# Two norm boundaries of a two-layer kernel in another order: three and four chunks token tile by token tile, three weight chunks split early, no subtraction on POOL

## The chip, the cores and the metric

The kernel runs on one core of a Trainium2 chip. The metric is the device time of one execution in microseconds (us), lower is better. The engines are TensorE (PE), VectorE (DVE), ScalarE (ACT), GpSimd (POOL) and SyncE (SP, which issues all DMAs here).

## What is computed

Two transformer-like layers on 256 tokens of width 2048, in fp32. Cut to what matters:

```python
# first block
h = rms_norm(x, norm_mix_pre)
proj = h @ w_in                        # 2048 x 10240
oa, on = diff_attention(...), neighbourhood_attention(...)
mixed = g_a * (oa @ w_branch_a) + g_b * (on @ w_branch_b)
x = x + rms_norm(mixed @ w_out, norm_mix_post)      # norm boundary 1
u = square(relu(rms_norm(x, norm_mlp_pre) @ w_up))  # 2048 x 8192
x = x + rms_norm(u @ w_down, norm_mlp_post)         # norm boundary 2
# second block
proj = rmsnorm(x, norm_w_2) @ w_in_2
h = x + concat(mlstm(...), hgrn2(...)) @ w_out_2
h = h + sigmoid(rmsnorm(h, pe_norm_w_2) @ w_pg_2) * (p @ w_pe_2)
out = rmsnorm(h, final_norm_w_2)
```

## The kernel before

**Chunks and halves.** All large products are cut into 340 chunks, numbered in the order in which they run. A chunk is four 128-row pieces of a weight matrix by 512 columns (344 in some): 1 MB. Tokens stand in two tiles of 128, t = 0 and 1. A block of chunks (4 of them for 2048 rows, 16 for w_down) sums into two PSUM buffers `acc`, one for each tile. `products(n)` runs chunk n for tile 0 and then for tile 1; such a part is called (n,t) or a half below. The stages start at chunks 0 (w_in), 80 (branches), 96 (w_out, `N_WO`), 112 (w_up, `N_UP`), 176 (w_down, `N_DN`), 240 (second w_in, `N_IN2`), 308, 324.

**fp32 from fp32r.** Each operand is split into a high part, which is a copy rounded to fp32r, and a low part, the difference. A half is 4 x 3 matmuls: hi x ath, lo x ath, hi x atl, where hi/lo belong to the weights and ath/atl to the activations.

**The weight pipeline.** SP loads chunk n into one of three `raw` buffers once the lo of chunk n-3 is made. ACT makes hi (`high(n)`, L461), DVE makes lo (`low(n)`, L811), both into one of three buffers that the products of chunk n-3 have left. ACT and DVE do this for chunk n+2 (`LEAD`) while chunk n runs. Eight lo are made on POOL (`POOL_LO`, L379): those of chunks 3 and 5, 114 to 116, 242 to 244.

**The norm boundaries.** After the last chunk of w_out (111) or w_down (239) the residual stream is renewed: ACT squares the last block (`square`), DVE sums and POOL takes the root (`row_mean`, `root`), DVE weighs the last block (`weigh_last`) and adds a quarter row of a tile at a time to `xs` (`add_row`, L799). Then come eight units (g, t), a group g of 512 columns of tile t: PE turns it around with four transpositions (L1252), DVE scales it by the norm's gain (`unit`, L791), ACT makes ath (L478) and DVE atl (`unit_low`, L836). Units are called r1 at boundary 1 and r2 at boundary 2. `fill` puts them one half ahead of the first chunks of the next stage: chunk 112+g needs units (g,0) and (g,1). Behind the first unit PE runs 16 short matmuls on constants (`warm`). Two chunks later ACT squares the whole rows for the next norm.

**w_down.** Its activations lie in `UT` (64 pieces of 256 columns in `m`). ACT and DVE split four pieces for each chunk (`cut(i)` for chunk 176+i, three chunks ahead).

**Order and waits.** Each engine runs a list written out by hand. Waits are on semaphores that count: a wait for one result is a wait for everything counted before it on that engine.

Of the kernel before, what the change touches and what calls it, by code (L numbers as in the profile page):

```python
# [15 lines left out]
P = 128  # L16
D = 2048
# [10 lines left out]
POOL_LO = {n + i for n in (N_UP, N_IN2) for i in (2, 3, 4)} | {3, 5}  # L28
# [41 lines left out]
def program(nc, x, w_in, w_a, w_b, w_out, w_up, w_down, w_in2, w_out2, w_pg, w_pe, p2,  # L70
            cols, lamv, rpb, rows, bif, cos_c, sin_c, nam_c, id_c, lvl_c, caus_c, out):
    with ExitStack() as ctx:
# [12 lines left out]
        M = sb("m", [P, 80 * KB])  # L85
        SM = sb("sm", [P, 3 * KB])
# [16 lines left out]
        s_plo = Count(sem("s_weights_lo_pool"))  # L103
# [6 lines left out]
        counts = [s_prod, s_pe, s_hi, s_lo, s_plo, s_ach, s_act, s_dve, s_pool, s_out, *s_raw]  # L110
# [103 lines left out]

        def freed(b):

            kind, j = blocks[b][:2]
            return s_dve if kind in on_dve or (kind, j) == ("dn", 3) else s_act

        def view(t, n):  # L220
            return t[n % NRAW][:, 0:4 * chunks[n][1]]

        def lo_done(n):
            return s_plo if n in POOL_LO else s_lo
# [46 lines left out]
        def fill(name, c0):  # L271
            order = [(g, t) for g in range(4) for t in range(2)]
            for i, u in enumerate(order):
                at = max(0, i - 1)
                before.setdefault((c0 + at // 2, at % 2), []).append((name, *u))

# [6 lines left out]
        fill("r1", N_UP)  # L283
        fill("r2", N_IN2)
# [9 lines left out]
        freeing = {"heads": N_AB - 4, "mix": N_WO - 4, "y": N_RES - 4, "pg": N_PG - 4}  # L294

        def taken(name, g):

            return {"r1": N_UP - 1, "r2": N_IN2 - 1}.get(name, freeing.get(name, 0) + g)
# [7 lines left out]
        def sync(e):  # L306
# [5 lines left out]
            def raw(n):  # L312
                if n >= NRAW:
                    sp.wait_ge(lo_done(n - NRAW), "lo", n - NRAW)
                e.dma_start(view(RAW, n).rearrange("p (k c) -> p k c", c=chunks[n][1]), chunks[n][0]).then_inc(
                    s_raw[n % NRAW].on("raw", n), 16)
# [19 lines left out]
            for n in range(3, N_ALL):  # L336
# [34 lines left out]
        def gpsimd(e):  # L371
            po = Queue(e)

            def low(n):
                hi, lo, raw = view(HI, n), view(LO, n), view(RAW, n)
                po.wait_ge(s_hi, "hi", n)
                if n >= NSPL:
                    po.wait_ge(s_prod, "products", n - NSPL, 1)
                e.tensor_tensor(lo, raw, hi.bitcast(F32), ALU.subtract).then_inc(s_plo.on("lo", n))  # L379

# [19 lines left out]
            for n in range(N_ALL):  # L400
                if n == 3:
                    root(2, 2, "r0")
                if n + LEAD in POOL_LO:
                    low(n + LEAD)
# [43 lines left out]
        def scalar(e):  # L448
# [8 lines left out]
            def high(n):  # L457
                if n >= NSPL:
                    ac.wait_ge(s_prod, "products", n - NSPL, 1)
                ac.wait_ge(s_raw[n % NRAW], "raw", n)  # L460
                e.activation(view(HI, n), view(RAW, n), ACT.Copy).then_inc(s_hi.on("hi", n))  # L461

            def unit(name, g, t):
                h = ATH[:, 4 * g:4 * g + 4, t * P:(t + 1) * P]
                if name == "heads":
                    ac.wait_ge(s_act, *(("da back", 7) if g < 2 else ("na out", 7)))
                    ac.wait_ge(s_prod, "products", taken(name, g), 1)
                    src = (QT if g < 2 else QN)[:, 4 * (g % 2):4 * (g % 2) + 4, t * P:(t + 1) * P]
                elif name == "mix":
                    ac.wait_ge(s_pe, "unit", name, g, t)  # L470
                    ac.wait_ge(s_prod, "products", taken(name, g), 1)
                    src = cut4(mis[:, place.get((name, g, t), 0), :])
                else:
                    ac.wait_ge(s_dve, "unit", name, g, t)
                    if name != "x":
                        ac.wait_ge(s_prod, "products", taken(name, g), 1)
                    src = cut4(STG[name][(2 * g + t) % 2])
# [141 lines left out]

            def evac(b):  # L620
                kind, j, n, ids = blocks[b]
                ps = [acc[:, 2 * (b % 2) + t, 0:n] for t in range(2)]
                for t in range(2):
# [16 lines left out]
                    if kind == "wo" or (kind, j) == ("dn", 3):  # L640
# [103 lines left out]
            for n in range(N_ALL):  # L744
                for t in range(2):
# [3 lines left out]
                if n + LEAD < N_ALL:  # L749
                    high(n + LEAD)  # L750
# [9 lines left out]
                if n in (N_UP + 3, N_IN2 + 3):  # L760
# [817 lines left out]
```

## Time and profile before

| | us |
|---|---|
| median of 3 runs | 2049.67 |
| lowest, highest | 2048.22, 2049.98 |
| profiled execution, own time | 2048.93 |
| its span in the trace | 2047.1 |
| PE busy | 2007.7 (98%) |
| DVE busy | 1180.9 (58%) |
| ACT busy | 981.8 (48%) |
| POOL busy | 77.2 (4%) |

Times in the views are counted from the start of the span. A line of the timeline gives start, duration, engine, source line, operation, out<-in, shapes, and in brackets the idle time of the engine before it and what ended that. Matmuls are pipelined: their durations overlap, so the distance of two starts tells their cost, not the duration.

### The profile page before, as it was taken

The numbers are of one execution on the slowest core, as the hardware profiler recorded it, in microseconds if no ns is written. First come the engines' busy times: TensorE is split into PE (matmuls) and PEld (weight loads), VectorE is DVE, ScalarE is ACT, GpSimd is POOL, SyncE is SP. The second block draws the span as 40 slices with busy tenths as digits, with TensorE's granted clock in tenths as the row PEclk, the third lists the DMA queues.
The fourth block names the chain that finished last, engine by engine and source line by source line (L and its number), as shares of the span: only waits on it lengthen the run. The fifth ranks groups of instructions, "written<-read, shape, count | busy, mean of one in ns | idle before, by whom it ended". The sixth has DMA issues, their size and how long they took to land.

```text
span 2047.1 us, 22415 instructions
## 1 busy us (share of the span) xinstructions
PE 2007.7 (98%) x9288; PEld 1664.1 (81%) x9288; DVE 1180.9 (58%) x1067; ACT 981.8 (48%) x956; POOL 77.2 (4%) x50
## 2 busy tenths in 40 slices
PE   7999999999999899999999999999999999999998
PEld 6888888888888688888888888887789888888776
DVE  5655546644655644444456666676567858676554
ACT  4335544445444354444455555553555445444443
POOL 2000000000000200000000000001100000230000
PEclk9999999999999999999999999999999999999999
DMA  6554455555646465656555555564446444465442
GB/s 229 201 199 145 164 188 183 174 185 188 223 164 206 124 193 183 185 185 189 183 181 203 186 196 195 185 226 144 165 144 207 165 152 152 133 221 191 158 166 108
DMA packets 184894, 366.79 MB, mean 179 GB/s; under 512 B 6616, under 2 KB 13400, under 8 KB 184152
## 3 DMA queue, kind: packets, MB, share of 16 engines
q1 hardware_dynamic: 184792, 365.36, 53.7%
q8 instruction: 73, 1.20, 0.2%
q14 instruction: 29, 0.24, 0.0%
HBM read 363.24 MB, written 2.10 MB: 178 GB/s over the span
## 4 chain that ended last, share of the span: by engine, by line
PE 95%; DVE 2%; issue 2%; ACT 1%; DMA 0%; POOL 0%; SPq 0%; DVEq 0%; POOLq 0%; ACTq 0%
PE acc L1249 88%; PE mis L1249 4%; PE mis L1252 3%; DVE xs L799 1%; DVE m L791 1%; DVE atl L836 0%; DMA xs<-in_x 0%; POOL lo L379 0%; ACT hi L461 0%; DVE xs L791 0%; ACT ath L478 0%; ACT sm L455 0%; ACT m L454 0%; SPq L310 0%; DVE m L799 0%
## 5 line engine op out<-in xcount | busy, mean ns | idle before, releaser
L811 DVE TENSOR_TENSOR lo<-raw,hi 128x2048 fp32r<-128x2048 f32 (+1 forms) x331 | 750.5, 2269 | 661.0 <-ACT hi L461 658.9
L1249 PE MATMUL acc<-hi,ath 128*128 128x512 f32 (+1 forms) x2720 | 1073.6, 395 | 8.9 <-DVE atl L836 8.9
L1249 PE MATMUL acc<-hi,atl 128*128 128x512 f32 (+1 forms) x2720 | 1056.7, 388 | 0.0
L1249 PE MATMUL acc<-lo,ath 128*128 128x512 f32 (+1 forms) x2720 | 1055.7, 388 | 0.0
L461 ACT ACTIVATE hi<-raw 128x2048 fp32r<-128x2048 f32 (+1 forms) x339 | 640.1, 1890 | 403.3 <-PE acc L1249 402.7
L1249 PEld LDWEIGHTS acc<-hi,ath 128*128 128x128 f32 x2720 | 513.0, 189 | 113.2 <-DVE atl L836 7.8
L1249 PEld LDWEIGHTS acc<-hi,atl 128*128 128x128 f32 x2720 | 512.6, 188 | 105.3
L1249 PEld LDWEIGHTS acc<-lo,ath 128*128 128x128 f32 x2720 | 513.4, 189 | 100.3 <-issue 0.5
L454 ACT ACTIVATE m<-mis 128x512 f32<-128x512 f32 (+1 forms) x96 | 50.3, 524 | 222.8 <-PE mis L1252 193.9
L454 ACT ACTIVATE m<-acc,st 128x512 f32<-128x512 f32 (+1 forms) x102 | 69.3, 679 | 112.4 <-PE acc L1249 109.4
L791 DVE TENSOR_TENSOR m<-m 128x512 f32<-128x512 f32 (+2 forms) x117 | 74.2, 634 | 22.8 <-ACT m L454 18.1
L1249 PE MATMUL mis<-m 128*128 128x128 f32 (+1 forms) x492 | 84.3, 310 | 0.0
L478 ACT ACTIVATE ath<-m 128x512 fp32r<-128x512 f32 x48 | 29.8, 629 | 113.0 <-DVE m L791 102.2
L843 DVE TENSOR_TENSOR atl<-m,ath 128x1024 fp32r<-128x1024 f32 x64 | 78.0, 1219 | 5.4 <-ACT ath L485 5.4
L384 POOL TENSOR_TENSOR st<-st,mhalf 128x1 f32<-128x1 f32 (+3 forms) x20 | 17.3, 863 | 1686.1 <-DVE st L795 1686.1
L1249 PEld LDWEIGHTS mis<-m 128*128 128x128 f32 x492 | 68.6, 191 | 4.7
L485 ACT ACTIVATE ath<-m 128x1024 fp32r<-128x1024 f32 x64 | 66.7, 1042 | 2.1 <-PE acc L1249 2.1
L454 ACT ACTIVATE m<-m 128x1024 f32<-128x1024 f32 (+3 forms) x34 | 36.0, 1058 | 62.0 <-DVE m L791 58.8
L1252 PE MATMUL mis<-idn,m 128*128 128x128 f32 x356 | 54.2, 272 | 4.3 <-DVE m L791 4.0
L1252 PEld LDWEIGHTS mis<-idn,m 128*128 128x128 f32 x356 | 44.3, 139 | 16.2 <-DVE m L791 4.4
L836 DVE TENSOR_TENSOR atl<-m,ath 128x512 fp32r<-128x512 f32 x48 | 43.7, 918 | 21.2 <-ACT ath L478 21.2
L791 DVE TENSOR_TENSOR m<-mis,col 128x512 f32<-128x512 f32 x40 | 27.6, 690 | 28.0 <-PE mis L1252 25.7
(108 smaller groups left out, 503.3 us busy)
## 6 DMA issues: line engine op xcount, KB each, us to landing
raw<-in_w_in SPq DMA_DIRECT2D x135, 1024.0 KB, 5.0
raw<-in_w_up SPq DMA_DIRECT2D x64, 1024.0 KB, 5.5
raw<-in_w_down SPq DMA_DIRECT2D x64, 1024.0 KB, 5.0
raw<-in_w_out SPq DMA_DIRECT2D x32, 1024.0 KB, 5.0
raw<-in_w_pg SPq DMA_DIRECT2D x16, 1024.0 KB, 5.0
raw<-in_w_in SPq DMA_DIRECT2D x12, 688.0 KB, 4.2
raw<-in_w_a SPq DMA_DIRECT2D x8, 1024.0 KB, 5.0
raw<-in_w_b SPq DMA_DIRECT2D x8, 1024.0 KB, 4.9
```

The lines of the kernel that those rows point to most:

```text
L384: e.tensor_tensor(ST[:, c:c + n], ST[:, c:c + n], MHALF[:, 0:n], ALU.pow).then_inc(s_pool.on(*name))
L454: return e.activation(o, i, f, scale=scale, bias=bias)
L461: e.activation(view(HI, n), view(RAW, n), ACT.Copy).then_inc(s_hi.on("hi", n))
L478: e.activation(h, src, ACT.Copy).then_inc(s_ach.on("ath", name, g, t))
L485: e.activation(ATH[:, 4 * (i % 4):4 * (i % 4) + 4, :], UT[:, 4 * (i % 16):4 * (i % 16) + 4, :], ACT.Copy).then_inc(s_ach.on("cut hi", i))
L791: return e.tensor_tensor(o, a, b, op)
L799: return e.scalar_tensor_tensor(o, a, s, b, op0, op1)
L811: e.tensor_tensor(lo, raw, hi.bitcast(F32), ALU.subtract).then_inc(s_lo.on("lo", n))
L836: e.tensor_tensor(l, src, h.bitcast(F32), ALU.subtract).then_inc(s_dve.on("atl", name, g, t))
L843: e.tensor_tensor(ATL[:, s4:s4 + 4, :], UT[:, k:k + 4, :], ATH[:, s4:s4 + 4, :].bitcast(F32), ALU.subtract).then_inc(s_dve.on("cut", i))
L1249: return e.matmul(o, a, b, start=start, stop=stop)
L1252: return e.transpose(o, a, IDN[:, :])
```

## The change

- At each boundary the seven chunks from three before the new stage to three behind its first (109 to 115, 237 to 243; `turning`) leave the chunk loops of PE, DVE and ACT. A function `turnover` on each engine writes their order out. On PE: tile 0 of the last three chunks, tile 1 of two of them, units (0,0), (1,0), (2,0), tile 1 of the last chunk; then tile 0 of the first four chunks of the new stage with units (3,0), (0,1), (1,1), (2,1), (3,1) between them; then tile 1 of these four. `warm` is gone.
- hi and lo of the new stage's first three chunks are made earlier, into memory in `m` that is free by then (`SPARE`): for 112 to 114 during chunks 100, 101, 102, for 240 to 242 during 231, 233, 236 (`EARLY`). Their loads move forward in SP's list with them. For 240 to 242 ACT waits until DVE has finished cut 53, 57 or 63, which read that memory.
- `raw` buffers go round in the new order of loads; hi/lo buffers go round among the chunks that are not early.
- No lo is made on POOL; DVE makes all.
- The squares of whole rows are taken tile by tile inside `turnover`; a unit waits for the tile of the old chunk that it overwrites, no longer for both.

```diff
-POOL_LO = {n + i for n in (N_UP, N_IN2) for i in (2, 3, 4)} | {3, 5}
+EARLY = {N_UP: (100, 101, 102), N_IN2: (231, 233, 236)}
...
+        ahead = {n: [n + LEAD] for n in range(N_ALL - LEAD)}
+        spare = {}
+        for first, when in EARLY.items():
+            for i, n in enumerate(when):
+                ahead[first + i - LEAD].remove(first + i)
+                ahead[n].append(first + i)
...
             def high(n):
-                if n >= NSPL:
-                    ac.wait_ge(s_prod, "products", n - NSPL, 1)
-                ac.wait_ge(s_raw[n % NRAW], "raw", n)
-                e.activation(view(HI, n), view(RAW, n), ACT.Copy).then_inc(s_hi.on("hi", n))
+                if split_before(n) is not None:
+                    ac.wait_ge(s_prod, "products", split_before(n), 1)
+                if N_UP <= n < N_UP + 3:
+                    ac.wait_ge(s_pe, "unit", "mix", 3, 1)
+                if N_IN2 <= n < N_IN2 + 3:
+                    ac.wait_ge(s_dve, "cut", (53, 57, 63)[n - N_IN2])
+                ac.wait_ge(s_raw[nth[n] % NRAW], "raw", n)
+                e.activation(hi_of(n), raw_of(n), ACT.Copy).then_inc(s_hi.on("hi", n))
...
+            def turnover(name, n0):        # ACT
+                b = chunks[n0 - 1][2]
+                high(n0 - 1)
+                square(b, 0)
+                high(n0 + 3)
+                unit(name, 0, 0)
+                unit(name, 1, 0)
+                unit(name, 2, 0)
+                square(b, 1)
+                unit(name, 3, 0)
+                row_square(name, 0)
+                high(n0 + 4)
...
+                row_square(name, 1)
+                high(n0 + 5)
+                ac.wait_ge(s_prod, "products", n0 + 2, 1)
+                evac(b + 1)
...
+                for c in ahead.get(n, ()):
+                    if c not in spare:
+                        high(c)
                 if N_DN <= n < N_IN2:
                     cut(n - N_DN + 3)
+                for c in ahead.get(n, ()):
+                    if c in spare:
+                        high(c)
...
-                if name in ("r1", "r2") and (g, t) == (0, 0):
-                    warm(16, number["up", 0] if name == "r1" else number["hf", 0])
...
+            def turnover(name, n0):        # PE
+                for c in range(n0 - 3, n0):
+                    products(c, 0)
+                products(n0 - 3, 1)
+                products(n0 - 2, 1)
+                unit(name, 0, 0)
+                unit(name, 1, 0)
+                unit(name, 2, 0)
+                products(n0 - 1, 1)
+                products(n0, 0)
+                unit(name, 3, 0)
+                products(n0 + 1, 0)
+                unit(name, 0, 1)
+                unit(name, 1, 1)
+                products(n0 + 2, 0)
+                unit(name, 2, 1)
+                products(n0 + 3, 0)
+                unit(name, 3, 1)
+                for c in range(n0, n0 + 4):
+                    products(c, 1)
```

DVE at boundary 1, from the lo of chunk 111 on, before. `st` holds the sums, `xs` is the residual stream, `m<-acc,m` is `weigh_last`, `m<-mis,col` is `unit`, `atl` is `unit_low`:

```order
285 L811 TENSOR_TENSOR lo<-raw,hi 128x2048 x3
286 L1089 TENSOR_REDUCE st<-st 128x1
287 L795 TENSOR_SCALAR st<-st 128x1
288 L791 TENSOR_TENSOR m<-acc,m 128x512
289 L799 SCALAR_TENSOR_TENSOR xs<-m,st,xs 128x512
290 L811 TENSOR_TENSOR lo<-raw,hi 128x2048
291 L1089 TENSOR_REDUCE st<-st 128x1
292 L795 TENSOR_SCALAR st<-st 128x1
293 L791 TENSOR_TENSOR m<-mis,col 128x512
294 L799 SCALAR_TENSOR_TENSOR xs<-m,st,xs 128x512
295 L836 TENSOR_TENSOR atl<-m,ath 128x4x128
296 L791 TENSOR_TENSOR m<-acc,m 128x512
```

And now, the same place:

```order
292 L862 TENSOR_TENSOR lo<-raw,hi 128x2048 x2
293 L1140 TENSOR_REDUCE st<-st 128x1
294 L848 TENSOR_SCALAR st<-st 128x1
295 L844 TENSOR_TENSOR m<-acc,m 128x512
296 L852 SCALAR_TENSOR_TENSOR xs<-m,st,xs 128x512 x4
297 L844 TENSOR_TENSOR m<-mis,col 128x512 x2
298 L887 TENSOR_TENSOR atl<-m,ath 128x4x128
299 L844 TENSOR_TENSOR m<-mis,col 128x512
300 L887 TENSOR_TENSOR atl<-m,ath 128x4x128 x2
301 L1140 TENSOR_REDUCE st<-st 128x1
302 L848 TENSOR_SCALAR st<-st 128x1
303 L844 TENSOR_TENSOR m<-acc,m 128x512
```

The additions of tile 0 now stand together ahead of any unit, and three units of tile 0 ahead of the second tile's sum; before, one addition stood before each unit, and the two tiles alternated.

ACT at boundary 2, from the hi of chunk 238 to the squares of the last block, before (`ath<-m 128x1024` is the cut's high part):

```order
444 L461 ACTIVATE hi<-raw 128x2048
445 L485 ACTIVATE ath<-m 128x1024
446 L461 ACTIVATE hi<-raw 128x2048 x3
447 L455 ACTIVATE sm,st<-acc 128x512 x2
448 L478 ACTIVATE ath<-m 128x4x128 x3
```

And now:

```order
452 L480 ACTIVATE hi<-raw 128x2048
453 L504 ACTIVATE ath<-m 128x1024
454 L480 ACTIVATE spare_54<-raw 128x2048
455 L480 ACTIVATE hi<-raw 128x2048
456 L470 ACTIVATE sm,st<-acc 128x512
457 L480 ACTIVATE hi<-raw 128x2048
458 L497 ACTIVATE ath<-m 128x4x128 x3
459 L470 ACTIVATE sm,st<-acc 128x512
```

The hi of chunk 242 (`spare_54`) now stands between the last cut and the hi of chunk 239, and the square of tile 1 behind three units of tile 0.

## Rows read from the trace of the kernel before

**Rows 1.** The page, part 1: busy time and share of each engine

```profile
PE 2007.7 (98%) x9288; PEld 1664.1 (81%) x9288; DVE 1180.9 (58%) x1067; ACT 981.8 (48%) x956; POOL 77.2 (4%) x50
```

**Rows 2.** Who waited for whom, engine PE: us in total, times, longest

```profile
PE mis L1252 <- DVE xs L799: 9.8, 6, 2.5
PE acc L1249 <- DVE atl L836: 8.9, 5, 2.3
```

**Rows 3.** Timeline of PE, boundary 1: start, us, what

```profile
682.24 0.39 PE L1249 MATMUL acc<-hi,atl 128*128 128x512 f32 x1
...
690.63 0.48 PE L1249 MATMUL acc<-hi,ath 128*128 128x512 f32 x1
...
693.85 0.48 PE L1249 MATMUL acc<-hi,ath 128*128 128x512 f32 x1
...
717.58 0.50 PE L1249 MATMUL acc<-hi,ath 128*128 128x512 f32 x1 [2.31 <-DVE atl L836]
...
725.88 0.60 PE L1252 MATMUL mis<-idn,m 128*128 128x128 f32 x4
```

**Rows 4.** Timeline of PE, boundary 2

```profile
1410.73 0.39 PE L1249 MATMUL acc<-hi,atl 128*128 128x512 f32 x1
...
1457.48 0.60 PE L1252 MATMUL mis<-idn,m 128*128 128x128 f32 x4
```

**Rows 5.** Stretches, boundary 2: us, busy PE PEld DVE ACT POOL, PEclk, DMA share, GB/s

```profile
1416.00:1421.00 5.00, 5.00 (x18) 3.90 (x19) 2.62 (x5) 0.63 (x1) 0.00 (x0) 0.66 0.36 137
```

**Rows 6.** The chain that ended last, an undisturbed piece: start, us, what

```profile
732.41 16.36 PE acc L1249 x72
```

**Rows 7.** The page, part 5: groups; busy us, mean ns of one, idle before

```profile
L811 DVE TENSOR_TENSOR lo<-raw,hi 128x2048 fp32r<-128x2048 f32 (+1 forms) x331 | 750.5, 2269 | 661.0 <-ACT hi L461 658.9
...
L461 ACT ACTIVATE hi<-raw 128x2048 fp32r<-128x2048 f32 (+1 forms) x339 | 640.1, 1890 | 403.3 <-PE acc L1249 402.7
...
L478 ACT ACTIVATE ath<-m 128x512 fp32r<-128x512 f32 x48 | 29.8, 629 | 113.0 <-DVE m L791 102.2
...
L791 DVE TENSOR_TENSOR m<-mis,col 128x512 f32<-128x512 f32 x40 | 27.6, 690 | 28.0 <-PE mis L1252 25.7
```

**Rows 8.** Timeline of DVE, boundary 1

```profile
680.66 0.16 DVE L1089 TENSOR_REDUCE st<-st 128x1 f32<-128x4 f32 x1 [4.64 <-ACT sm L455]
...
681.85 0.75 DVE L799 SCALAR_TENSOR_TENSOR xs<-m,st,xs 128x512 f32<-128x512 f32 x1
...
686.63 0.69 DVE L836 TENSOR_TENSOR atl<-m,ath 128x512 fp32r<-128x512 f32 x1
...
694.85 4.42 DVE L799 SCALAR_TENSOR_TENSOR xs<-m,st,xs 128x512 f32<-128x512 f32 x1
```

**Rows 9.** Timeline of DVE, boundary 2: the last cut

```profile
1393.56 1.22 DVE L843 TENSOR_TENSOR atl<-m,ath 128x1024 fp32r<-128x1024 f32 x1
```

**Rows 10.** The page, part 6: DMA issues, KB each, us to landing

```profile
raw<-in_w_up SPq DMA_DIRECT2D x64, 1024.0 KB, 5.5
```

**Rows 11.** DMA view of 1360 to 1400 in 40 slices of 1 us

```profile
GB/s 2 0 150 379 410 111 0 74 299 408 268 0 12 131 399 418 96 0 47 301 408 293 0 45 215 395 377 33 0 102 334 408 205 0 45 250 403 348 2 0
```

**Rows 12.** The start: timeline of POOL, DVE and PE, the chain, a stretch

```profile
30.16 4.56 POOL L379 TENSOR_TENSOR lo<-raw,hi 128x2048 fp32r<-128x2048 f32 x1 [28.62 <-ACT hi L461]
...
30.63 4.64 DVE L836 TENSOR_TENSOR atl<-m,ath 128x512 fp32r<-128x512 f32 x1 [0.83 <-ACT ath L478]
...
47.13 3.43 DVE L791 TENSOR_TENSOR m<-m 128x256 f32<-128x256 f32 x2
...
52.24 0.89 DVE L791 TENSOR_TENSOR m<-m 128x256 f32<-128x256 f32 x2
...
50.62 0.66 PE L1252 MATMUL mis<-idn,m 128*128 128x128 f32 x4 [3.96 <-DVE m L791]
...
51.27 7.06 PE acc L1249 x24
...
53.00:56.00 3.00, 3.00 (x11) 2.40 (x10) 3.00 (x3) 0.70 (x1) 0.00 (x0) 0.68 0.41 157
```

More of the change, by code:

```diff
@@ L269, in program @@
         before, behind = {}, {}
[L271 to L275, printed above, removed]
         def fill_early(name, e0, last):
@@ L312, in raw @@
             def raw(n):
[L313 to L316, printed above, removed]
+                if nth[n] >= NRAW:
+                    sp.wait_ge(s_lo, "lo", order[nth[n] - NRAW])
+                e.dma_start(raw_of(n).rearrange("p (k c) -> p k c", c=chunks[n][1]), chunks[n][0]).then_inc(
+                    s_raw[nth[n] % NRAW].on("raw", n), 16)
             load(XS[:, 0, 0:512], xv[:, 0, 0:512], "x", 0, 0)
@@ L335, in sync @@
             load(BIF[:, :], bif, "bif")
-            for n in range(3, N_ALL):
+            for n in order[3:]:
                 if n == 25:
@@ L759, in scalar @@
                         act(m(48, 2048), XS[:, t, :], ACT.Square, accum=ST[:, t:t + 1]).then_inc(s_act.on("x sq", t))
-                if n in (N_UP + 3, N_IN2 + 3):
-                    for t in range(2):
-                        y = Y if n < N_DN else Y2
-                        ac.wait_ge(s_dve, "added", "r1" if n < N_DN else "r2", 3, t)
-                        ac.wait_ge(s_dve, "atl", "r1" if n < N_DN else "r2", 3, 1)
-                        act(y[:, t, :], XS[:, t, :], ACT.Square, accum=ST[:, 50 + t:51 + t]).then_inc(s_act.on("xr sq", n, t))
                 b = chunks[n][2]
@@ L819, in unit @@
                 if name in SCALE:
[L820 removed]
+                    z = cut4(stage(name, g, t))
                     c0 = SCALE[name] + 4 * g
@@ L1210, in vector @@
                 last = n == blocks[chunks[n][2]][3][-1]
-                if n + LEAD < N_ALL and not (n in (N_UP - 1, N_IN2 - 1)):
-                    low(n + LEAD)
+                for c in ahead.get(n, ()):
+                    if c not in spare:
+                        low(c)
                 if N_DN <= n < N_IN2:
                     cut(n - N_DN + 3)
+                for c in ahead.get(n, ()):
+                    if c in spare:
+                        low(c)
                 units(behind.get(n, ()))
@@ L1483, in tensor @@
             for n in range(N_ALL):
-                products(n)
+                if n in turning:
+                    if n + 3 in EARLY:
+                        turnover("r1" if n < N_UP else "r2", n + 3)
+                    continue
+                for t in range(2):
+                    for u in before.get((n, t), ()):
+                        if u[:2] != ("x", 0):
+                            unit(*u)
+                    products(n, t)
                 for u in behind.get(n, ()):
```

189 lines of the change are left out of this document (112 added, 77 removed).

## The prediction, made before the changed kernel ran

> **What bounds the kernel now.** I read the page first. TensorE is busy for 98% of the span [rows 1], so only the moments in which it is not fed can be won. The list of who waits for whom puts 9.8 us of its idle time on the residual addition (xs, L799) and 8.9 us on the low part of the activations (atl, L836) [rows 2]. The timeline of PE says where: a stage's last matmul starts at 682.24, the first transposition behind chunk 116 at 725.88, and one of the waits between them is seen at 717.58, 2.31 us for atl [rows 3]. The same stretch at the second norm boundary runs from 1410.73 to 1457.48 [rows 4], and there the granted clock falls to a mean of 0.66 in 1416 to 1421, a mixture of its two levels, 1.2 and 2.4 GHz [rows 5]. Away from the boundaries 72 matmuls take 16.36 us [rows 6], 0.2272 us each: a half (one chunk with one token tile, 12 matmuls) is 2.73 us, a chunk 5.45 us. DVE and ACT have slack there: 2.27 us to make a chunk's lo, 1.89 us to make its hi [rows 7], of 5.45.
>
> **Boundary 1, term 1.** Call T the start of chunk 109. It is 71 matmuls before 682.24: 666.1. The last transposition of the stretch starts at 725.88 [rows 3], so chunks 109 to 116 now take 59.8 us. 192 matmuls at 0.2272 are 43.6. The eight transpositions of the new order stand in five groups; a group of four costs 0.49 (the halves on its two sides start at 690.63 and 693.85, 3.22 apart, not 2.73 [rows 3]); eight of them would be 3.9, and I put 3.8, since the groups of 12 and 8 start up only once. Without a wait the stretch is 47.4 us: 12.4 us to win.
>
> Does a wait remain? I lay the new DVE and ACT order out from T with the durations of the rows. From the end of a half to the row sum on DVE is 0.9 us (half (111,0) ended by 679.75, the reduction starts at 680.66), the first addition (from 681.85) ends 2.85 after the half [rows 8]; an addition is 0.75, scaling by the gain 0.69, ath 0.63, atl 0.69 [rows 7, 8].
> - (111,0) is now due at T+5.5, not T+10.9. Its hi can start when (108,1) ends, at T+0.2; lo is done at T+4.4. Slack 1.1.
> - (111,0) ends at T+8.2; additions of tile 0 end at 11.0, 11.8, 12.5, 13.2. The twelve transpositions stand at T+13.6, behind (109,1) and (110,1). Slack 1.1.
> - atl of group 0 is done near 16.4; (112,0) is due at 17.7. Groups 1 and 2 are done by 18.5, due at 20.9 and 24.4.
> - The second tile's chain starts when (111,1) ends, at 17.7; its additions are done by 21.3 (two) and 23.4 (four). The transpositions that need the first two stand at 23.6.
> - lo of chunk 115 follows on DVE at 24.1 and ends at 26.4; (115,0) is due at 27.6. Slack 1.2.
> - atl of tile 1: 28.6, 29.3, 33.0, 35.1, due at 30.8, 33.5, 36.2, 39.0.
> - lo 116 ends at 32.3 (due 41.7), lo 117 at 40.8 (due 47.6), and the evacuation of the first up block is over by 42.5, before chunk 118 wants anything.
> No wait: the whole 12.4 us counts. The reason that it fits is that the norm of tile 0 runs under three halves of tile 1, and that three chunks' hi and lo are already there.
>
> **Boundary 2, term 2.** T is 1410.73 less 71 matmuls, 1394.6. To 1457.48 it is 62.9 us, so 15.5 to win, the low clock included. One wait appears. ACT now makes the hi of chunk 242 before that of 239, and only once DVE has done the last cut. Before, that cut starts at 1393.56 and takes 1.22 [rows 9]: hi 242 runs 1394.9 to 1396.7, hi 239 to 1398.6; on DVE lo 242 is over at 1399.0 and lo 239 at 1401.3. But (239,0) is now due at T+5.45, 1400.05. TensorE waits 1.3 us. Term 2 is 14.2.
>
> **The early chunks.** Each adds nothing in sum (hi 1.89, lo 2.27 are moved, not added), but each takes a raw buffer and a 1 MB transfer out of turn. Around chunks 100 to 102 six transfers are wanted in 16.3 us. A transfer lands 5.5 us after issue [rows 10], but its data moves at up to 410 GB/s in slices of 1 us [rows 11], so one needs 2.6 us of the DMA engines and two overlap. By that, raw 104 lands at 630 instead of before 628, lo 104 is done near 634 and due at 639. Around 231, 233 and 236 the same account has each raw there before ACT asks. I take zero. The bound from the other side is transfers that do not overlap at all, 5.5 each: then about 3 us are lost behind chunk 104, and raw 239, fifth in a row behind raw 241 (1377), lands at 1404.5, for a wait of 8.7 us in place of 1.3. The value is nearest to the slices of rows 11, which show the bandwidth itself. A gain here is excluded: nothing waited for these chunks' data.
>
> **Start, term 3.** The subtractions of chunks 3 and 5 leave POOL. While POOL makes lo 3 (4.56 us from 30.16), an atl on DVE takes 4.64 us instead of 0.69; while it makes lo 5, two small DVE operations of the rope (at 47.13) take 3.43 instead of 0.89 [rows 12]. TensorE waits 3.96 us at 50.62 for the latter; the clock then has a mean of 0.68 in 53 to 56, and the 24 matmuls from 51.27 take 7.06 us [rows 12]. After: DVE makes lo 3 from 30.16 to 32.4 (hi 3 is there when POOL starts), scaling, ath and atl follow, and atl ends at 34.4 instead of 35.3 (30.63 plus 4.64); everything behind is 0.87 earlier, the rope additions start near 46.2 and end at 47.15. The transposition moves from 50.62 to 47.2: 3.4 us. The gap of TensorE shrinks from 4 to 1.5 us. If the clock then stays at its upper level, the 24 matmuls take 5.45 instead of 7.06: 1.6 more. The 36 matmuls behind the wait of 2.31 us at 717.58 fill the time to 725.88 [rows 3], 8.3 us for 8.2 undisturbed, so there was no such loss; behind 3.96 us there was; 1.5 is nearer to the former, so I count it. Term 3 is 5.0, with 3.4 as its lower end.
>
> **POOL and warm-ups.** While a lo ran on POOL, an addition on DVE took 4.42 us instead of 0.75 [rows 8]. There are three such lo at each boundary; they are a large part of what terms 1 and 2 win, and with none on POOL the loss can't come back. Dropping 16 warm-up matmuls per boundary is worth nothing by itself: they lay in a wait for the second addition. Their cover, keeping the array active, is needed only if a long wait stays.
>
> **Sum.** 12.4 + 14.2 + 5.0 = 31.6. The profiled execution's own time is 2048.93: 2017.3. The median of the runs is 0.7 above it, so the forecast for the median is 2018.0.
>
> **A rule that speaks against it.** In the trace a group of four transpositions between two halves costs 0.49 us and nothing behind it [rows 3]. The new order has twelve in one go, some 1.3 us. The Trainium skill, "TensorE: Matmul & The Clock Gate", part 4 on PE-mode transpose, says that transposes do not count as activity for the clock the way matmuls do. By that each boundary has a stretch that counts as idle, the clock may fall behind it, and the sum would be that of the first rival. No row here has twelve transpositions in a row, so the trace neither confirms nor refutes it.
>
> **Rivals.**
> - The clock falls behind the short gaps and the twelve transpositions. A fall costs 1.6 us, as behind 51.27 [rows 12]. Once at the start and once per boundary: 4.8, 2023. For: the fall in 1416 to 1421 [rows 5]. Against: that one follows a long wait, and behind 717.58 there is none.
> - Weight starvation as bounded above: 0 to 3 at the first boundary, 0 to 7.4 more at the second, 6 in all if it shows: 2024.
> - The hand-laid chains miss their slack of 1.1 to 1.3 us. If each of a dozen handovers costs 0.15 more than I took, 0.7 is lost at two or three places of each boundary, and a fall of the clock may follow: 2 x (1.8 + 1.6) = 7, 2025.
> - The change doesn't do what it says: semaphores count in order, so a wait for one early result is a wait for all queued before it. If that undoes the overlap of the tiles, only POOL's share and the start stay, about half: 2033.
> - Slower than before: the array is at its lower level throughout both new orders, since no warm-ups lead into them. At 1.2 GHz a half takes up to twice its 2.73 us. The gain of 31.6 is used up at 12 halves; the new orders have 28, and 20 of them at the lower level give 2018 + 55 = 2073. Against: the mean of 0.66 over 5 us, right behind the longest wait [rows 5], says that the lower level did not even last that long.
>
> **How the numbers follow.** Forecast as summed 0.62; clock 0.09; starvation 0.10; missed slack 0.13; undone 0.04; slower 0.02. The range: below, the 1.3 us wait may not appear and T's accounts may be off by a microsecond or two: 2014.5. Above, it takes in the clock, starvation and missed slack to a little over their middles: 2027. What is left out is about 0.15: the far ends of these, and the last two cases. A difference of 0.2%, 4 us, is about what can be told from none. Faster 0.96, same 0.02, slower 0.02.
>
> **What the profile after would show.** Terms 1 and 2: no idle time of PE with a releaser from chunk 109 to 116, the span of these chunks at 47 to 48 us, no atl or addition over 0.8 us on DVE. Term 2: one PE wait of 1 to 1.5 us for lo, two halves into the last three chunks of the down projection. Term 3: the first rope transposition near 47.2 and the clock at 1.00 behind it. Starvation: ACT's hi waiting for a DMA behind chunks 102 and 241, PE waiting for lo soon after. Wrong as a whole: a PE wait over 3 us in either new stretch.

## The result, and the profile after

| | before | after |
|---|---|---|
| median of runs on the same chip (4 and 4), us | 2049.64 | 2017.2 |
| lowest, highest | 2048.22, 2049.98 | 2016.85, 2017.28 |
| profiled execution, own time | 2048.93 | 2017.24 |
| its span in the trace | 2047.1 | 2015.5 |

The recorded ratio of the runs is 0.9849, 95% interval 0.9837 to 0.9862: 1.5% faster (the quotient of the two medians above is 0.9842). The forecast was 2018.0.

The page of the kernel after, part 1 [rows 1 of before]: busy us, share of the span, instructions.

```profile
PE 1992.3 (99%) x9256; PEld 1655.0 (82%) x9256; DVE 1175.5 (58%) x1075; ACT 981.9 (49%) x956; POOL 40.6 (2%) x42
```

PE has 32 instructions fewer (two times 16 warm-ups) and 15.4 us less busy time, which includes the 32 warm-ups and the stretches of slow clock. POOL has eight instructions fewer and 36.6 us less busy time.

Who waited for whom, engine PE, after [rows 2]: us in total, times, longest. Source lines moved: the residual addition is now L852, atl L887, lo L862.

```profile
PE acc L1325 <- DVE atl L887: 3.8, 4, 1.4
...
PE acc L1325 <- DVE lo L862: 1.1, 1, 1.1
```

The 9.8 us for residual additions are gone, atl is down from 8.9 to 3.8, and one wait is new, 1.1 us for a lo. The timeline of PE after, boundary 1 [rows 3]:

```profile
674.76 1.47 PE L1328 MATMUL mis<-idn,xs 128*128 128x128 f32 x12
675.99 0.48 PE L1325 MATMUL acc<-hi,ath 128*128 128x512 f32 x1
...
708.39 0.60 PE L1328 MATMUL mis<-idn,m 128*128 128x128 f32 x4
```

and boundary 2 [rows 4]:

```profile
1383.83 0.50 PE L1325 MATMUL acc<-hi,ath 128*128 128x512 f32 x1 [1.07 <-DVE lo L862]
...
1392.13 1.47 PE L1328 MATMUL mis<-idn,xs 128*128 128x128 f32 x12
...
1425.75 0.60 PE L1328 MATMUL mis<-idn,m 128*128 128x128 f32 x4
```

Five halves, 60 matmuls of 0.2267 us, stand ahead of the twelve transpositions, so chunk 109 starts at 661.16 and the stretch to 708.39 is 47.2 us long. At the second boundary chunk 237 starts at 1377.16: that is 1392.13 less 60 matmuls (13.6), less the wait (1.07) and less 0.3 that the stop and the restart cost besides. That stretch is 48.6 us.

The stretches of both boundaries and of the start, after: us, busy PE PEld DVE ACT POOL, granted clock, DMA share, GB/s.

```profile
660.00:712.00 52.00, 52.00 (x248) 43.27 (x247) 31.26 (x38) 23.27 (x25) 1.78 (x3) 1.00 0.39 116
1376.00:1430.00 54.00, 52.93 (x251) 43.72 (x250) 34.61 (x46) 26.19 (x28) 1.78 (x3) 1.00 0.41 137
40.00:60.00 20.00, 18.61 (x87) 15.09 (x86) 14.46 (x14) 10.68 (x10) 0.78 (x1) 1.00 0.61 213
```

PE is busy for all of the 52 us of boundary 1, and the granted clock is 1.00, the upper level of 2.4 GHz, in all three stretches. At the start, the timeline of PE and the chain of work that ended last (before: [rows 12]) say

```profile
47.17 0.66 PE L1328 MATMUL mis<-idn,m 128*128 128x128 f32 x4 [1.39 <-DVE m L844]
...
47.84 5.48 PE acc L1325 x24
```

| part | before | after | gained | forecast |
|---|---|---|---|---|
| to the start of chunk 109 | 666.1 | 661.2 | 5.0 | 5.0 (term 3) |
| chunks 109 to 116 | 59.8 | 47.2 | 12.5 | 12.4 (term 1) |
| chunks 237 to 244 | 62.9 | 48.6 | 14.3 | 14.2 (term 2) |
| span | 2047.1 | 2015.5 | 31.6 | 31.6 |

The three parts add up to 31.8 us; the rest of the span is 0.2 longer. That the forecast is met to 0.1 us in this pair of traces is in part luck. The kernel before, run again on other chips beside the experiments, scatters from 2045.93 to 2050.49 us, and on the chip of x9_after (below) the medians of the two kernels are 30.0 us apart (2047.34 and 2017.39), here 32.4. The terms came out right as sums; the experiments ask whether their reasons were.

### The profile page after: what moved, and what is told of

Its sections match the earlier page's. It is cut to its first block, busy times and chain, and to the rows that moved or that the text cites. A ratio compares the mean times of both kernels' runs of the same rounds, so it can differ in the third digit from the quotient of the medians.

```text
span 2015.5 us, 22345 instructions
## 1 busy us (share of the span) xinstructions
PE 1992.3 (99%) x9256; PEld 1655.0 (82%) x9256; DVE 1175.5 (58%) x1075; ACT 981.9 (49%) x956; POOL 40.6 (2%) x42
## 4 chain that ended last, share of the span: by engine, by line
PE 95%; ACT 2%; DVE 1%; issue 1%; DMA 0%; SPq 0%; POOL 0%; DVEq 0%; ACTq 0%
PE acc L1325 89%; PE mis L1325 4%; PE mis L1328 2%; ACT hi L480 1%; DVE m L844 1%; DMA raw<-in_w_in 0%; ACT ath L497 0%; DVE atl L887 0%; DVE lo L862 0%; DVE xs L844 0%; SPq L334 0%; ACT m L470 0%; ACT m L469 0%; ACT spare L480 0%; DVE m L852 0%
## 5 line engine op out<-in xcount | busy, mean ns | idle before, releaser
L862 DVE TENSOR_TENSOR lo<-raw,hi 128x2048 fp32r<-128x2048 f32 (+1 forms) x333 | 754.9, 2269 | 645.4 <-ACT hi L480 643.1
L1325 PE MATMUL acc<-hi,ath 128*128 128x512 f32 (+1 forms) x2672 | 1050.0, 393 | 4.9 <-DVE atl L887 3.8
L1325 PE MATMUL acc<-hi,atl 128*128 128x512 f32 (+1 forms) x2672 | 1034.7, 387 | 0.0
L1325 PE MATMUL acc<-lo,ath 128*128 128x512 f32 (+1 forms) x2672 | 1033.4, 387 | 0.0
L480 ACT ACTIVATE hi<-raw 128x2048 fp32r<-128x2048 f32 (+1 forms) x333 | 628.8, 1890 | 380.6 <-PE acc L1325 374.5
L1325 PEld LDWEIGHTS acc<-hi,ath 128*128 128x128 f32 x2672 | 501.9, 188 | 105.6 <-issue 5.4
L1325 PEld LDWEIGHTS acc<-hi,atl 128*128 128x128 f32 x2672 | 501.5, 188 | 102.4
L1325 PEld LDWEIGHTS acc<-lo,ath 128*128 128x128 f32 x2672 | 502.1, 188 | 98.0 <-issue 0.5
L887 DVE TENSOR_TENSOR atl<-m,ath 128x512 fp32r<-128x512 f32 x48 | 34.2, 714 | 20.8 <-ACT ath L497 20.4
L844 DVE TENSOR_TENSOR m<-mis,col 128x512 f32<-128x512 f32 x40 | 27.6, 690 | 15.7 <-PE mis L1328 13.4
```

The lines of the kernel that those rows point to most:

```text
L480: e.activation(hi_of(n), raw_of(n), ACT.Copy).then_inc(s_hi.on("hi", n))
L844: return e.tensor_tensor(o, a, b, op)
L887: e.tensor_tensor(l, src, h.bitcast(F32), ALU.subtract).then_inc(s_dve.on("atl", name, g, t))
L1325: return e.matmul(o, a, b, start=start, stop=stop)
```

## The experiments

In the trace a stretch is counted as above: from the start of chunk 109 (or 237) to the first transposition behind chunk 116 (244).

**Theory.** POOL's lo slows DVE's operations, and that costs by itself only about 2 us per boundary. The long idle times come from the row sum, addition, transposition chain of each tile. Early chunks free DVE and ACT during it; tile by tile order gives TensorE work during it; the start stands alone. Rivals: POOL is nearly the whole gain; or it costs nothing at the boundaries; or the early chunks starve the weights.

### Part by part

**x1_dve_lo.** The kernel before, every lo on DVE.

```diff
-POOL_LO = {n + i for n in (N_UP, N_IN2) for i in (2, 3, 4)} | {3, 5}
+POOL_LO = set()
```

> The kernel before, with every lo on DVE and nothing else changed. Theory (the lock between a lo on POOL and two-input operations of DVE cost 3.7, 1.9 and 2.9 us in three places of each boundary, but three lo on DVE put 2.2 us each back into the same chain): about 1.9 us gained per boundary and 5.0 at the start, 2041. Rival (the lock was the whole loss, and the lo find room on DVE): 8.5 per boundary and 5.0, 2027. Second rival (DVE is the bound there, serial lo cost as much as the lock): 2044.6.

Measured: 2035.35 us (2034.82 to 2035.7), ratio 0.9934 (0.992 to 0.9947), span 2033.0, 14.1 less than before. The theory's number is too high by 6 us, the second rival's by 9, and the first rival's is too low by 8. The stretches are 57.4 and 55.8 us (before 59.8 and 62.9), the start gives 4.8. The waits, engine PE:

```profile
PE mis L1252 <- DVE xs L799: 7.0, 6, 1.7
PE acc L1249 <- DVE atl L836: 5.9, 5, 1.4
```

and two windows of it, boundary 1 just behind the second addition, and all of boundary 2:

```profile
682.00:687.00 5.00, 4.96 (x16) 3.74 (x17) 3.22 (x5) 0.63 (x1) 0.00 (x0) 0.66 0.50 171
1390.00:1450.00 60.00, 55.10 (x264) 43.98 (x263) 38.09 (x47) 28.47 (x30) 1.79 (x3) 1.00 0.42 138
```

Most of the missing 6 us is the clock. In the traced execution of the kernel before it falls once in boundary 1 and three times in boundary 2; beside the one of [rows 5] there are these:

```profile
700.00:705.00 5.00, 5.00 (x17) 3.99 (x18) 2.05 (x3) 2.43 (x2) 1.75 (x1) 0.66 0.67 204
...
1447.00:1452.00 5.00, 4.37 (x12) 3.50 (x13) 2.95 (x3) 4.01 (x4) 0.10 (x2) 0.66 0.76 243
```

The third of boundary 2 is the chain's piece of 12 matmuls from 1430.03 that takes 4.55 us instead of 2.97. In this kernel's trace one of the four falls is left. At about 1.6 us each (4.55 less 2.97, the same piece at the upper level at 687.47), three falls are 4.8 us. The rest, 14.1 less 4.8 for the start and less 4.8, is 4.5 us for both boundaries: what POOL costs by itself is 2.2 each, near the 1.9 of the theory.

**x2_start.** The kernel before, only chunks 3 and 5 taken from POOL.

```diff
-POOL_LO = {n + i for n in (N_UP, N_IN2) for i in (2, 3, 4)} | {3, 5}
+POOL_LO = {n + i for n in (N_UP, N_IN2) for i in (2, 3, 4)}
```

> The kernel before, with only the lo of chunks 3 and 5 moved from POOL to DVE. Theory: term 3 alone, 3.4 for the wait ahead of the first rope transposition and 1.6 for the clock behind it, 2044.6, and the boundaries as before. Rival: the clock falls behind the shorter gap too, 2046.2.

Measured: 2044.97 (2042.67 to 2046.91, 10 runs), ratio 0.9981 (0.9972 to 0.999), span 2042.2, 4.9 less. The timeline of PE and the chain:

```profile
47.16 0.66 PE L1252 MATMUL mis<-idn,m 128*128 128x128 f32 x4 [1.43 <-DVE m L791]
...
47.82 5.49 PE acc L1249 x24
```

In the trace term 3 is what it was said to be: 3.5 us of wait and 1.6 of clock (5.49 us for 24 matmuls, 7.06 before). The runs are less sharp. The medians of this kernel and the kernel before on this chip (2048.51) are 3.5 us apart, and the interval reaches from 2.0 to 5.7 us, so they do not tell 5.0 from the lower end of 3.4.

The boundaries of this kernel are those of the kernel before, and its trace shows that the place of the falls varies from execution to execution. It has two falls at each boundary, one of them behind the wait of 2.3 us that had none in [rows 3]:

```profile
712.00:717.00 5.00, 4.40 (x13) 3.50 (x14) 2.92 (x3) 4.01 (x4) 0.10 (x1) 0.66 0.74 235
```

Its stretches are 61.3 and 61.3 us, where the trace of the kernel before has 59.8 and 62.9. The sum is the same; how it divides into terms 1 and 2 was a matter of the execution that was traced.

**x3_early_only.** The kernel after, but PE, DVE and ACT keep the order of before at the boundaries, with the 16 warm-ups: early chunks and no lo on POOL. Its difference from the kernel before, at the core:

```diff
+EARLY = {N_UP: (100, 101, 102), N_IN2: (231, 233, 236)}
...
-                if n + LEAD in POOL_LO:
-                    low(n + LEAD)
...
-            for n in range(3, N_ALL):
+            for n in order[3:]:
```

> The changed kernel with the old order at both boundaries (chunk by chunk, units and additions alternating between the tiles, 16 warm-up matmuls), but with the early hi and lo of three chunks and no lo on POOL. Theory: what is left of the loss is the norm's latency behind the last product, some 3.3 us per boundary, and the wait for the lo of chunk 239 is gone (1.2): 2022.6, with one fall of the clock 2024. So the tile order is worth 5 to 7 us and the early chunks some 18. Rival (the tile order is the greater part): 2030 or more.

Measured: 2028.63 (2027.94 to 2029.71), ratio 0.9902 (0.9888 to 0.9915), span 2027.0. That lies between the theory (2022.6 to 2024) and its rival (2030 or more): the theory missed by 4.6 us. The tile order is worth some 11 us and not 5 to 7, yet it is not the greater part of the whole gain either, as the rival had it. Both stretches are 53.3 us and the clock is 1.00 in both:

```profile
660.00:720.00 60.00, 57.23 (x273) 46.15 (x272) 32.92 (x38) 23.13 (x25) 1.79 (x3) 1.00 0.30 91
1380.00:1440.00 60.00, 57.19 (x273) 46.14 (x272) 34.94 (x39) 25.94 (x28) 1.78 (x3) 1.00 0.35 118
```

The pieces of the chain in boundary 1 show what I had missed:

```profile
692.50 0.63 ACT ath L505
693.13 1.81 ACT hi L488
...
695.00 2.17 issue
...
697.90 0.76 DVE xs L865
```

The first three chunks of the stage are early, the fourth is not. In the old order its hi comes behind a unit's ath on ACT, its lo waits for that hi on DVE (it runs under the 2.17 us of "issue"), and the next addition is queued behind the lo: TensorE waits 1.00 us at 698.71, and 1.36 at 706.93 for the same with the next chunk.

```profile
698.71 0.66 PE L1358 MATMUL mis<-idn,xs 128*128 128x128 f32 x4 [1.00 <-DVE xs L865]
...
706.93 0.50 PE L1355 MATMUL acc<-hi,ath 128*128 128x512 f32 x1 [1.36 <-DVE atl L900]
```

The ladder before, x1, x3, after, by stretches, divides the gain:

| step | start | boundary 1 | boundary 2 |
|---|---|---|---|
| no lo on POOL | 4.8 | 2.3 | 7.0 |
| early chunks | | 4.2 | 2.6 |
| tile by tile, no warm-ups | | 6.0 | 4.7 |

The first two rows hold the clock: of the 7.0 some 4.8, of the 4.2 some 1.6. As the place of the falls varies, the columns of the boundaries hold for these executions; their sums are surer. The starts of x1 and x3 differ by 0.7 us, with the time at which the first load of x lands. Over both boundaries the order of the tiles is the largest step, 10.7 us, against 9.3 for POOL (4.5 without the clock) and 6.8 for the early chunks (5.2 without it, 2.6 per boundary). The steps were added to one another in one order only; what each is worth in another was not measured. Tile order without early chunks wasn't tried: four chunks of the new stage are then under way at once, and there are three pairs of hi/lo buffers.

### The one wait that is left

**x4_late242.** The kernel after; chunk 242 is split behind 239 instead of ahead of it.

```diff
-EARLY = {N_UP: (100, 101, 102), N_IN2: (231, 233, 236)}
+EARLY = {N_UP: (100, 101, 102), N_IN2: (231, 233, 237)}
...
+                if name == "r2":
+                    high(n0 + 2)
...
+                if name == "r2":
+                    low(n0 + 2)
```

> The changed kernel with hi and lo of chunk 242 made behind those of chunk 239 (and loaded behind it). Theory: the one PE wait in the new stretch at boundary 2, for the lo of chunk 239, is gone and nothing comes in its place: 1.2 us faster, 2016.0. Rival (the additions of tile 0 then start late on DVE, or ACT reaches hi of chunk 243 late): no change, 2017.2.

Measured: 2016.44 (2015.87 to 2016.83), ratio 0.9841 (0.9828 to 0.9855), span 2014.9. To have the kernel after and this one on one chip, both were run again.

**x9_after** is the kernel after, unchanged.

> The changed kernel itself, run again beside the next ones so that they have it on the same chip: 2017.2, within 0.7.

**x4b_late242** is x4_late242, unchanged.

> Hi and lo of chunk 242 behind those of 239 once more, beside the changed kernel on one chip. Theory: the wait of 1.1 to 1.2 us at the new stretch of boundary 2 is gone and nothing else changes: 1.1 below the changed kernel. Rival: a start that waits longer for the first loads eats it up in some executions, no difference that can be told.

Measured: x9_after 2017.39 (2016.88 to 2017.56), ratio 0.985 (0.9835 to 0.9865), span 2015.8; x4b_late242 2015.84 (2015.64 to 2016.28), ratio 0.9844 (0.9827 to 0.986), span 2013.9. The two ranges don't touch: the medians are 1.55 us apart, 0.08%. In the trace the wait for lo is gone, and the stretch of boundary 2 is 47.2 us instead of 48.6. DVE in the kernel after, and in x4b_late242:

```profile
1379.28 2.29 DVE L862 TENSOR_TENSOR spare<-raw,spare 128x2048 fp32r<-128x2048 f32 x1 [1.98 <-ACT spare L480]
1381.49 2.28 DVE L862 TENSOR_TENSOR lo<-raw,hi 128x2048 fp32r<-128x2048 f32 x1
```

```profile
1379.13 2.29 DVE L864 TENSOR_TENSOR lo<-raw,hi 128x2048 fp32r<-128x2048 f32 x1 [2.01 <-ACT hi L480]
```

In the first the lo of 239 is the second of the two and TensorE waits for it; in the other it is the first. The mechanism behind the 1.3 of term 2 is right, and this version is the fastest measured here.

### Are the weights near starving?

**x10_dense.** The kernel after; the three early chunks of boundary 1 are all taken during chunk 100.

```diff
-EARLY = {N_UP: (100, 101, 102), N_IN2: (231, 233, 236)}
+EARLY = {N_UP: (100, 100, 100), N_IN2: (231, 233, 236)}
```

> The changed kernel with all three early chunks of boundary 1 made during chunk 100, so that four transfers of 1 MB stand in a row ahead of the load of chunk 103. Theory (transfers overlap, one follows the other by 2.6 us): raw 103 lands near 624.8, lo 103 is done 0.6 after TensorE is ready for it: 2017.9. Rival (they do not overlap, 5.5 us each): raw 103 lands at 628.2 and TensorE waits 4 us, 2021.2.

Measured: 2019.29 (2019.05 to 2019.6), ratio 0.986 (0.9845 to 0.9874), span 2017.8: 1.9 above x9_after on the same chip, between the theory and its rival. PE's new wait, and ACT's starts in the same kernel:

```profile
630.78 0.50 PE L1325 MATMUL acc<-hi,ath 128*128 128x512 f32 x1 [1.75 <-DVE lo L862]
```

```profile
623.06 1.92 ACT L480 ACTIVATE spare<-raw 128x2048 fp32r<-128x2048 f32 x1 [2.55 <-DMA raw<-in_w_up]
626.49 1.92 ACT L480 ACTIVATE hi<-raw 128x2048 fp32r<-128x2048 f32 x1 [1.51 <-DMA raw<-in_w_out]
629.75 1.91 ACT L480 ACTIVATE hi<-raw 128x2048 fp32r<-128x2048 f32 x1 [1.34 <-DMA raw<-in_w_out]
```

Each start waits for a load that just landed, and they are 3.3 to 3.4 us apart. I had taken 2.6, the theory's rival 5.5. What sets the 3.3 to 3.4 is not the DMA engines alone. SP issues a load only when the lo of the load three places ahead of it is made, and its queue shows the issue of the load that ACT takes up at 623.06, and the one that had to wait for that buffer:

```profile
617.60 0.37 SPq L339 DMA_DIRECT2D raw<-in_w_up  x1
...
627.32 0.37 SPq L339 DMA_DIRECT2D raw<-in_w_out  x1
```

Once round, from load (5.5 us) over hi and lo to the next load, takes 9.7 us here, and with three `raw` buffers that alone makes 3.2 us per load. The DMA engines are full in 621 to 627 (384 GB/s, a share of 1.0) and not in 627 to 629 (198 GB/s, 0.66). The kernel after waits there for loads as well, as here:

```profile
622.72 1.92 ACT L480 ACTIVATE spare<-raw 128x2048 fp32r<-128x2048 f32 x1 [2.38 <-DMA raw<-in_w_up]
```

but no wait of TensorE comes of it. Moving one early chunk forward by one chunk and one by two uses up the reserve.

### POOL while DVE is in the chain

**x5b_pool_busy.** The kernel after, with work added that has no use: at each boundary POOL makes two subtractions of 128x1024 in memory that is free then, behind the root for tile 0. (x5_pool_busy, meant to do the same in a buffer of its own, has no time, because SBUF has no room for that buffer.)

```diff
+                        if t == 0:
+                            z = m(76 if n < N_DN else 40, 1024)
+                            for _ in range(2):
+                                po.wait_ge(s_pool, LAST)
+                                e.tensor_tensor(z, z, z, ALU.subtract).then_inc(s_pool.on())
```

> The changed kernel with two subtractions of 128x1024 on POOL (some 2.3 us each), on memory that nothing else uses then, right behind the root for tile 0 at each boundary. No data depends on them. Theory (an operation of DVE with two SBUF inputs can't run while POOL has one): the four additions of tile 0 are held up by 2.3 to 4.6 us, the twelve transpositions are due with 1.1 to spare, so 1.2 to 3.4 us more at each boundary, 2019.6 to 2024.0, and DVE's additions show durations of over 2 us. Rival (in the kernel before it was the late data of POOL's lo, not a lock, that cost the time): 2017.2 and additions of 0.75 us.

Measured: 2019.95 (2019.71 to 2020.4), ratio 0.9863 (0.9847 to 0.988), span 2018.5. POOL, then DVE of this kernel; the last row is DVE of the kernel after.

```profile
671.76 4.20 POOL L442 TENSOR_TENSOR m<-m 128x1024 f32<-128x1024 f32 x2
...
671.90 6.17 DVE L857 SCALAR_TENSOR_TENSOR xs<-m,st,xs 128x512 f32<-128x512 f32 x4
```

```profile
671.42 3.12 DVE L852 SCALAR_TENSOR_TENSOR xs<-m,st,xs 128x512 f32<-128x512 f32 x4
```

Four additions take 3.05 us more while POOL works 4.2 us. Their slack is 1.1, so a part reaches TensorE:

```profile
675.24 0.60 PE L1333 MATMUL mis<-idn,xs 128*128 128x128 f32 x4
676.56 1.44 PE L1333 MATMUL mis<-idn,xs 128*128 128x128 f32 x8 [0.72 <-DVE xs L857]
```

From the first transposition to the first behind the stretch it is 34.9 us at both boundaries (675.24 to 710.18, 1393.94 to 1428.88), where x9_after has 33.6. That is 2.6 for two, and the spans differ by 2.7. No data hangs on this work of POOL, so it is POOL's running itself that slows DVE. The new order does not hide all of it, and that speaks for taking lo off POOL; the new order with the real lo of the boundaries on POOL was not run. No clock fall followed.

**x6_pool_start.** The kernel after, lo of chunks 3 and 5 back on POOL.

```diff
+            def low(n):
+                hi, lo, raw = hi_of(n), lo_of(n), raw_of(n)
+                po.wait_ge(s_hi, "hi", n)
+                po.wait_ge(s_prod, "products", split_before(n), 1)
+                e.tensor_tensor(lo, raw, hi.bitcast(F32), ALU.subtract).then_inc(s_plo.on("lo", n))
...
+                if n + LEAD in (3, 5):
+                    low(n + LEAD)
```

> The changed kernel with the lo of chunks 3 and 5 on POOL again. Theory: term 3 undone, 5.0 us slower, 2022.2: the wait ahead of the first rope transposition is 4 us again, and the 24 matmuls behind it take 7.1 us instead of 5.5. Rival (the clock fell there by chance): 3.4 slower, 2020.6, with 5.5 for the 24.

**x7_pool_start_warm.** The same with 30 matmuls on constants ahead of the first rope transposition, so that TensorE is not idle while it waits.

```diff
+                        if (kind, j, t) == ("rope", 0, 0):
...
+                            for _ in range(30):
+                                mm(mis[:, w, 0:S], RST[:, 0:P], RST[:, :], True, True)
```

> As the kernel with the lo of chunks 3 and 5 on POOL, with 30 matmuls of 128x256 on constants in TensorE's list ahead of the first rope transposition, which it otherwise waits for idle; they take some 3.5 of the 4 us. Theory: the clock stays up, the 24 matmuls behind take 5.5 us, 1.6 less than without them, 2020.6. Rival (what is slow there is not the clock but contention): 2022.2 and 7.1 us for the 24.

Measured: 2021.41 (2020.75 to 2023.43), ratio 0.9873 (0.986 to 0.9887), span 2021.6, and 2021.76 (2021.65 to 2022.26), ratio 0.9874 (0.986 to 0.9887), span 2020.0. PE's timeline and the chain, x6 first, then x7:

```profile
51.67 0.72 PE L1342 MATMUL mis<-idn,m 128*128 128x128 f32 x4 [3.96 <-DVE m L856]
...
52.40 7.03 PE acc L1339 x24
```

```profile
47.55 3.45 PE L1339 MATMUL mis<-rst 128*128 128x256 bf16 x30
51.65 0.66 PE L1342 MATMUL mis<-idn,m 128*128 128x128 f32 x4 [0.65 <-DVE m L856]
...
52.30 5.48 PE acc L1339 x24
```

The transposition starts at the same time, DVE being as late, and the clock is the only difference: 7.03 against 5.48 us. In the trace the 1.6 us of term 3 are shown. In the medians they are not: those of x6 and x7 don't differ, so the runs bear out neither the theory of x7 (1.6 less than x6) nor, by x6 alone, that the fall comes every time. The profiled execution of x6 is the slowest of its four (2023.43; two others took 2020.75 and 2020.77). Whether the clock falls in each of the others, or the first load of x (waits of 4.5 and 4.2 us) evens it out, stays open. Against the kernel after both are slower by 4.2 to 4.6 us in the medians, which come from different chips, and by some 4.9 in the ratios (0.9873 and 0.9874 against 0.9849 and 0.985). That is term 3 within its range of 3.4 to 5.0.

### The warm-ups

**x8_no_warm.** The kernel before without the 16 matmuls per boundary.

```diff
-                if name in ("r1", "r2") and (g, t) == (0, 0):
-                    warm(16, number["up", 0] if name == "r1" else number["hf", 0])
```

> The kernel before without the 16 warm-up matmuls at each boundary. Theory (they lie in a wait of 4 us for the second addition, and the falls of the clock come all the same, behind other waits too): 2049.6, within 2. Rival (they hold the clock up): the first chunks of both stages start at the lower level every time, 1.6 to 3 us more, 2052.

Measured: 2050.88 (2049.15 to 2053.47, 11 runs), ratio 1.0015 (1.0006 to 1.0024), span 2047.4. On this chip the kernel before has 2048.01, so the warm-ups were worth 2.9 us in the medians (1.2 to 4.9 by the interval), not nothing; that is the rival's answer. In the traces the two stretches together are 2.1 us longer (62.9 and 61.9), and five falls stand there in place of four. PE at the second addition of boundary 1:

```profile
684.77 1.12 PE L1252 MATMUL mis<-idn,xs 128*128 128x128 f32 x4 [3.46 <-DVE xs L799]
...
686.12 0.63 PE L1249 MATMUL acc<-lo,ath 128*128 128x512 f32 x1
686.54 0.63 PE L1249 MATMUL acc<-hi,atl 128*128 128x512 f32 x1
```

Starts 0.43 apart instead of 0.23 are the lower level, 1.2 GHz; the kernel before has its first fall of this boundary only at 700, and there TensorE is idle for 1.71 us while it waits for the second addition, not 3.46. As to their removal in the change, I had named the condition under which it costs (a long wait that stays), and no such wait stayed.

## Why the prediction was right, point by point

- **Term 1, 12.4: right as a sum.** PE runs without idle time through the stretch, 47.2 us against 47.4 laid out. The twelve transpositions cost 1.23 us (674.76 to 675.99), 0.41 for four.
- **The slack laid out by hand: right.** The additions of tile 0 end at 674.5, T + 13.4, where T + 13.2 was laid out; the transpositions stand at T + 13.6. lo of chunk 115 starts at 685.38, T + 24.2, where 24.1 was laid out:

```profile
685.38 2.28 DVE L862 TENSOR_TENSOR lo<-raw,hi 128x2048 fp32r<-128x2048 f32 x1
```

- **Term 2, 14.2: right, with its wait.** TensorE waits for lo two halves into the stretch, as laid out, and x4_late242 removes it. It is idle for 1.1 us, and the stretch is 1.4 longer than that of boundary 1; 1.3 was forecast. That this term was larger than term 1 depends on the execution that was traced: its 15.5 us of loss held three falls of the clock, those of term 1 one, and x2_start has two at each boundary.
- **Term 3, 5.0: right in the traces.** 1.4 us of wait left (1.5 forecast), the transposition at 47.17 (47.2), clock 1.00 behind it. The medians of x2, x6 and x7 leave 3.4 to 5.0 open.
- **The reasons given for the clock: one row misread, the outcome in part luck.** The fall in 1416 to 1421 was said to follow the longest wait. It follows one of 1.70 us, behind the warm-ups, and the same wait at boundary 1 has no fall behind it:

```profile
1415.25 0.66 PE L1252 MATMUL mis<-idn,xs 128*128 128x128 f32 x4 [1.70 <-DVE xs L799]
...
686.77 0.66 PE L1252 MATMUL mis<-idn,xs 128*128 128x128 f32 x4 [1.71 <-DVE xs L799]
```

  So the rows did not bear out that a gap of 1.5 us at the start is safe because 2.31 us once were. It did turn out so: in the kernel after and in eight of the experiments a wait of about 1.4 us stands at that place, and each time the 24 matmuls behind it take 5.47 to 5.49 us.
- **"POOL is a large part of terms 1 and 2": about a third, and half of that by way of the clock.** No lo on POOL gives 9.3 of the 26.8 us of both boundaries (2.3 and 7.0), some 4.8 of these from falls of the clock that no longer follow. The theory of x1_dve_lo, which took 1.9 us per boundary from the slowed additions, missed the falls behind them.
- **The early chunks cost nothing: right, on less ground than I gave.** I took 2.6 us of the DMA engines per load; loads in a row land 3.3 to 3.4 us apart. The account left out that a load waits for one of three buffers, which by itself made it one load in 3.2 us in x10_dense. ACT waits for loads, which the prediction had named as a sign of starvation, but TensorE doesn't, and x10_dense shows how little is missing: 1.9 us are lost with one load moved forward by a chunk and one by two. The rival of starvation was nearer than its price suggested.
- **"Warm-ups are worth nothing by themselves": wrong for the kernel before (2 to 3 us), without effect on the sum**, since the waits that they covered are gone.
- **The rule that spoke against it.** The clock stays at 1.00 over 660 to 712 and 1376 to 1430, behind both groups of twelve transpositions. The Trainium skill, "TensorE: Matmul & The Clock Gate", part 4 on PE-mode transpose, says that transposes do not count as busy the way matmuls do. That made a fall possible there. A run of 1.23 us of transpositions, even behind a wait of 0.72 us in x5b_pool_busy, did not bring one. Whether a longer one would, no run here shows.
- **Rivals.** Clock falls: none in the new orders. Missed slack: none. Undone: no, PE works through. The estimate for that rival, 2033, is close to x1_dve_lo's 2035.35, which is the case that it described: POOL's share and the start alone.

The medians differ by 32.4 us and the spans by 31.6; the rest is within the scatter of the kernel before (2048.22 to 2049.98).

## What to carry to other kernels

Where a reduction over all columns closes a stage, run the token tiles staggered across the boundary: one tile's norm then lies under the other tile's matmuls, and over both boundaries that was the largest single step here. It needs the next stage's first weights to be split already, and their loads spread out where the buffers and the DMA engines have room. When a wait is priced, add the chance of a fall of the clock behind it, of about 1.6 us here, and look for work on POOL beside DVE's chain.

## What the runs showed of the hardware that I had not expected

**The same wait does not always bring the clock down.** In the kernel before, the same instruction waits 2.31 us at boundary 1 with no fall behind it (36 matmuls in 8.3 us, [rows 3]), and 2.30 us at boundary 2 with one:

```profile
1447.63 0.79 PE L1249 MATMUL acc<-hi,ath 128*128 128x512 f32 x1 [2.30 <-DVE atl L836]
1448.22 0.63 PE L1249 MATMUL acc<-lo,ath 128*128 128x512 f32 x1
```

In x1_dve_lo the same wait of 1.71 us comes at both boundaries, with a fall behind the first (0.66 in 682 to 687) and none behind the second; in the kernel before it is the other way round. In x2_start both waits of 2.3 us have a fall and both of 1.7 have none. So over waits of 1.7 to 2.3 us the length of the wait and its place in the program don't decide it; what does is open. The wait of 2.5 us for an addition (in the kernel before at 699.33 and 1429.37) had a fall behind it all six times (both boundaries of the kernel before, x2_start and x8_no_warm). In the new orders of the boundaries the longest wait is 1.1 us, and no fall followed. The trace of the kernel before has four falls at the boundaries and one at the start, some 8 of the 31.6 us that the change gained, and a count of idle time doesn't show them.

**A slowed operation is slowed by most of the time that POOL shares with it.** In the kernel before an addition of 0.75 us that starts at 694.85 takes 4.42 [rows 8], 3.7 more, and POOL's lo runs for 3.9 us beside it:

```profile
694.16 4.56 POOL L379 TENSOR_TENSOR lo<-raw,hi 128x2048 fp32r<-128x2048 f32 x1 [8.48 <-ACT hi L461]
```

In x5b_pool_busy four additions take 3.05 us more, with POOL at work for 4.1 us beside them.

**Loads of 1 MB in a row** land 3.3 to 3.4 us apart in x10_dense (ACT's starts at 623.06, 626.49, 629.75), though the data of one moves at up to 412 GB/s in slices of 1 us, which would be 2.6 us. Two limits meet there: the DMA engines, full in 621 to 627, and the round of three buffers, 9.7 us, which gives a load in 3.2 us. No run with more buffers tells them apart.
